# State space tiles: VectorE scales the rows of the next tile before it updates the state

## What is computed

```python
def ssd_scan(x, dt, a, bm, cm, h0, chunk):
    ...
    xd = (x.astype(f32) * dt[..., None])...
    acs = jnp.cumsum(la, axis=2)
    lmat = jnp.exp(jnp.where(incl[:, :, None, None], acs[:, :, :, None] - acs[:, :, None, :], -jnp.inf))
    cb = jnp.einsum('bcign,bcjgn->bcijg', cc, bc)
    y_diag = jnp.einsum('bcijgr,bcjgrp->bcigrp', cb[..., None] * lmat, xd)
    states = jnp.einsum('bcjgn,bcjgrp->bcgrpn', bc, xd * jnp.exp(acs[:, :, -1:] - acs)[..., None])
    def step(h, inp):
        s, d = inp
        return d[..., None, None] * h + s, h
    ...
    y_off = jnp.einsum('bcign,bcgrpn->bcigrp', cc, h_prev) * jnp.exp(acs)[..., None]
    return (y_diag + y_off)..., h_fin...
```

## Time and profile before

| | |
|---|---|
| median of 3 runs | 3017.64 us (3016.84 to 3018.11) |
| the profiled execution | 3013.33 us |
| its span | 3011.5 us |
| TensorE products busy | 2650.2 us, 88% of the span |
| VectorE busy | 1265.4 us, 42% |
| ScalarE busy | 940.2 us, 31% |
| GpSimd busy | 904.5 us, 30% |
| the stage of the state space tiles | from about 160 to 260 us |

### The profile page before, as it was taken

The page is one execution under the profiler, slowest core; times in us unless marked ns, Lnnn a source line. Parts: engine busy times, 40 slices in busy tenths (PEclk is TensorE's granted clock), DMA queues, the critical chain, the costliest instruction groups (busy, mean ns, idle before and its releaser), DMA issues. The chain is left out here.

```text
span 3011.5 us, 47221 instructions
## 1 busy us (share of the span) xinstructions
PE 2650.2 (88%) x19663; PEld 2397.8 (80%) x19663; DVE 1265.4 (42%) x2531; ACT 940.2 (31%) x1719; POOL 904.5 (30%) x449
## 2 busy tenths in 40 slices
PE   5778889988989999978878787879998889899998
PEld 5745888655889999977867686769996569899997
DVE  5764411576343222253755375442104552522224
ACT  4242221465352212152322333222214543412122
POOL 2241221133254333352233133213321003633331
PEclk9987989899999999988988898889999989999998
DMA  4202255441222222222201020102322172222221
GB/s 147 73 15 77 77 93 132 147 214 51 57 56 85 85 84 85 84 75 61 73 15 31 30 74 15 30 17 84 92 80 79 33 211 81 67 81 78 82 84 60
DMA packets 217570, 232.93 MB, mean 77 GB/s; under 512 B 40780, under 2 KB 186668, under 8 KB 216750
## 3 DMA queue, kind: packets, MB, share of 16 engines
q1 hardware_dynamic: 215278, 229.66, 24.9%
q10 hardware_dynamic: 2080, 0.25, 0.1%
HBM read 207.93 MB, written 48.35 MB: 85 GB/s over the span
## 5 line engine op out<-in xcount | busy, mean ns | idle before, releaser
L271 POOL TENSOR_TENSOR WRr<-WR,WH 128x2048 fp32r<-128x2048 f32 (+3 forms) x98 | 443.3, 4523 | 828.8 <-ACT WH L259 828.8
L2206 PE MATMUL PS<-HHr,WRr 128*128 128x288 f32 x1104 | 327.9, 297 | 0.0
L411 PE MATMUL PS<-HHr,WH 128*128 128x288 f32 (+1 forms) x928 | 278.3, 300 | 49.5 <-PEq L97 49.5
L411 PE MATMUL PS<-YTr,WRr 128*128 128x288 f32 x1024 | 304.4, 297 | 0.0
L259 ACT CAST WH<-WR 128x2048 fp32r<-128x2048 f32 (+3 forms) x98 | 180.5, 1842 | 347.3 <-DMA WR<-in_mlp_w 188.1
L411 PE MATMUL PS<-YTr,lt_WX 128*128 128x288 f32 x1408 | 281.8, 295 | 0.0
L411 PE MATMUL PS<-HHr,WRr 128*128 128x288 f32 (+1 forms) x928 | 277.8, 299 | 0.0
L411 PE MATMUL PS<-HTr,WH 128*128 128x288 f32 (+1 forms) x928 | 277.7, 299 | 0.0
L271 POOL TENSOR_TENSOR WRr<-WR,lt_WX 128x2048 fp32r<-128x2048 f32 x35 | 162.0, 4629 | 234.1 <-ACT lt_WX L259 234.1
L411 PE MATMUL PS<-WH,HHr 128*128 128x256 f32 (+3 forms) x760 | 220.8, 291 | 13.0 <-PEq L97 13.0
L411 PEld LDWEIGHTS PS<-YTr,lt_WX 128*128 128x128 f32 x1408 | 227.3, 189 | 0.1
(11 more groups left out here) (663 smaller groups left out, 6150.4 us busy)
## 6 DMA issues: line engine op xcount, KB each, us to landing
WR<-in_mlp_w SPq DMA_DIRECT2D x64, 1024.0 KB, 5.3
WR<-in_cd_w_in SPq DMA_DIRECT2D x34, 1024.0 KB, 5.4
out_dil_s<-in_cache_dil_kv SPq DMA_DIRECT2D x2, 7936.0 KB
WR<-in_ab_w_in SPq DMA_DIRECT2D x10, 1024.0 KB, 5.3
past_rows<-in_cache_nsa_kv SPq DMA_DIRECT2D x16, 256.0 KB, 3.4
WR<-in_ab_w_in SPq DMA_DIRECT2D x16, 256.0 KB, 4.2
WR<-in_nsa_ck_w SPq DMA_DIRECT2D x4, 1024.0 KB, 5.3
WR<-in_nsa_cv_w SPq DMA_DIRECT2D x4, 1024.0 KB, 5.7
```

Source lines behind the costliest of these rows:

```text
L271: pool.tensor_tensor(K.WRr[:, n % RING, 0:used], K.WR[:, n % RING, 0:used], high_slot(K, i, used).bitcast(F32), ALU.subtract).then_inc(K.l ...
L411: last = pe.matmul(out, a, b, start=(n == 0), stop=(n == 3 * len(terms) - 1))
L2206: last = pe.matmul(out, a[:, k, c], h[:, k, x], start=(n == 0), stop=(n == 3 * KT - 1))
```

## The change

In VectorE's loop over the tiles, the two calls at its end change places:

```diff
@@ -1217,8 +1217,8 @@
                         if t + 1 < TT:
                             times_cb(t + 1, 3)
                         if t < NT:
+                            rows(t + 1)
                             state(t)
-                            rows(t + 1)
```

## The result

The median went from 3017.64 to 3028.60 us, 7 runs each: a ratio of 1.0034 with a 95% interval of 1.0024 to 1.0044. The change makes the kernel slower, by 7 to 13 us, and the predicted 3027.3 lies 1.3 us from the median.

What follows compares the result with a forecast made beforehand. TensorE's order of work was taken to bound the state space tiles' stage. First pieces +9.12, second -5.75, clock +7.5 and last tile -1.2 gave +9.7 us, 3023.0 for the profiled execution and a median of 3027.3; range 3020 to 3034.

Steps and rivals of the forecast that it cites:

- The wait that takes over: TensorE's L1051 waits for the state (d_H), idle some 6.7 us in tile 1 and 7.9 in tiles 2 and 3.
- The first piece: From the transposes to the first masked product: 9.40 us in tile 1, 10.65 in tiles 2 and 3, together +9.12.
- The scalings: VectorE's two scalings and Btok take 4.32 us until its next instruction, VectorE starting ahead of GpSimd in every tile.
- The second piece: From the first masked product to the last broadcast sum: 4.45 us a tile at full clock, saving 5.75 us.
- The clock term: TensorE's clock falls to half in each gap of tiles 1 to 3, costing 2.50 us a tile, +7.5 us.
- Rival 1: The clock costs nothing new, as TensorE runs one dense burst after the wait: +2.2 us, 3019.8; chance 0.19.
- upper bound of 6.7 us a tile: Most the clock could cost each of tiles 1 to 3, if the period stays at half clock throughout.
- rival 3: The clock stays low from L1051 to each period's end in three tiles: +22.3 us, 3039.9; chance 0.12.
- The last tile: No L1051 waits for the state there, so scaling starts 0.43 us earlier and takes 0.80 less: -1.2 us.
- The sum: The stage's terms together, 9.12 - 5.75 + 7.5 - 1.2 = +9.7 us, giving a median of 3027.3 us.
- a change of time outside of the stage: Sign that the prediction is wrong: the change was to act in the state space tiles' stage only.

Runs made afterwards that it cites:

- e11: The changed kernel with GpSimd's d_YD waiting for Btok and unused products of ones in TensorE's gaps: 3010.48 us, ratio 0.9979.
- e10: The kernel before with GpSimd's d_YD waiting for Btok and unused products of ones in TensorE's idle time: 2999.41 us, ratio 0.9938.
- e2: The changed kernel with unused products of ones on TensorE behind the transposes, to hold the clock: 3017.61 us, ratio 0.9996 to the kernel before.
- e6: The changed kernel with GpSimd's d_YD waiting for Btok, not for the copied rows: 3024.77 us, ratio 1.0010 to the kernel before.
- e8: The changed kernel again, unaltered, for a second profile and more times: 3026.09 us, ratio 1.0018 to the kernel before.
- e1: The kernel before with the new order in the last tile only: 3022.50 us, ratio 1.0004.
- e3: The kernel before with unused products of ones in TensorE's idle time, to hold the clock: 3008.98 us, ratio 0.9970.
- e7: The kernel before with an added stage of four chained VectorE products behind the tiles, as a pause: 3032.87 us, ratio 1.0039.
- e4: The changed kernel with TensorE's first four masked products ahead of C times B in tiles 1 to 3: 3028.99 us, ratio 1.0033 to the kernel before.
- e9: The changed kernel with four masked products ahead of C times B and unused products of ones in TensorE's gaps: 3011.71 us, ratio 0.9973 to the kernel before.

## Why the prediction was right

**The wait that takes over** was right as put: L1051 waits for the state and names d_H, 6.66 and 7.92 us where 6.7 and 7.9 were forecast, and L1082's wait for Btok is gone but for the last tile. e11 against e10 shows it by itself.

**The first piece** was right to the tenth where the clock is full: 9.40 and 10.65 forecast, 9.33 and 10.62 in e2. The trace of the change has 10.64 and 11.93, the same with 1.3 us of half clock in it.

**The scalings** were right: VectorE first, L1185 1.23 and L1186 2.80 in tiles 1 to 4. The rule of the Trainium skill (SBUF — State Buffer, Who interferes with whom) agrees whoever starts first: VectorE's L1185 kept its 1.23 and d_YD stretched to 2.94 after the change, L1185 stretched to 2.63 and d_YD kept its 1.90 before. L1204 in e6, which started first and kept its 1.22, is one more case.

**The second piece** was forecast at -5.75 for the full clock. From the masked products to the last sum it is 4.34 in e2 in all three tiles, so -6.08 against the 4.45, 7.70 and 6.95 of before; in the trace of the change it is 4.74, 4.73 and 4.73, with some half clock in it.

**The clock term was mis-sized.** The sum had 2.50 us a tile, 7.5 in all; against e2 it was 1.71, 1.71 and 1.70, 5.1 in all, and 5.75 in e8. The 2.50 was read from tile 3 of before, where the clock came back only after the second group of masked products. After the change it is back within the first group (at about 191.9, 215.8 and 239.7), 3.5 us after L1051 began. What the Trainium skill says of idle gaps (TensorE: Matmul & The Clock Gate, HAM oscillation — how this bites in real kernels) agrees: behind the gap each burst starts at half clock, tile 1's new as well, with L1051 at 1.22 us instead of the 0.71 of e2.

Rival 1 held that L1051, a broadcast sum and the masked products, coming in one piece behind the wait, bring the clock back soon. That this was the reason is not shown: in e6 they come in one piece too, behind a gap of 6.34 us, and the clock was back only 4.9 and 5.9 us after L1051 began, in tiles 2 and 3, at a price of 2.40 and 2.84 us (periods of 23.00 and 23.45 against 20.60 and 20.61 in e11). So 2.50 is a price that this order of work can meet; why it was less after the change stays open.

The upper bound of 6.7 us a tile, on which rival 3 rests, was too low: it left out that VectorE's L1195 waits for TensorE's L1089. From the last sum to the end of L1089 it is 3.69 us in tile 1 before (192.26 to 195.95), and at half clock about 7.2 by an estimate from these rows, which would hold L1195 back by 2.6 us (it began 4.61 behind the sum) where the bound had 0.8: some 8.5 us a tile. No run kept the clock down for so long.

**The last tile** was right: -1.2 forecast, 17.29 - 16.08 = 1.2 measured between its transposes and L1296, and the same in e1.

**The sum** for the stage, with what was measured in its terms: +8.98 for the first pieces (9.33, 10.62 and 10.61 in e2 against 6.79, 7.75 and 7.04), -6.08, +5.12 for the clock and -1.21 make +6.8, which is what the stretch grew by; in e8 it grew by 7.5. The forecast said +9.7. The first measurement of the times has +11.0 (7.2 to 13.3), the second +3.4 by the medians and +5.4 by the ratio (0.6 to 10.0). Both intervals hold the forecast of 9.7, the first lies just above the 6.8 of the stretch and the second holds it, so the times can't tell the two apart. That 3027.3 came out 1.3 us from the median is luck: the stage brought 2.9 us less than forecast, and 4.1 us outside of it happened to come on top.

The prediction had named a change of time outside of the stage as a sign against it. The profiles show one: less the stretch, the span is 2931.8 us before, 2940.1 after and 2937.2 in e8. But it is 2943.2 in e1, 2936.3 in e3 and 2945.3 in e7, which keep the order of before in tiles 1 to 3, so the sign doesn't tell the change from other executions and doesn't count against the mechanism.

## What to carry to other kernels

When two pieces of work of one engine change places, ask for each which wait it ends and what stands ahead of the freed work in the queue of the engine that waits: here the masked products, which looked free to go, stood behind one that needed the state. Put the less urgent piece where its engine idles anyway, and take the time of the urgent one from what it contends with; one moved wait on GpSimd gave 6.6 us in the stage, and the swap lost 6.8. Judge changes of this size by a stretch of the profile, since the times of this kernel scatter by more.

## What the runs showed of the hardware that was not expected

- Products whose results nobody reads, put into TensorE's gaps, kept the clock of tiles 2 and 3 of the change at 1.00 where it was 0.79 (e2), and made the stage 8.3 us shorter in the order of before (79.66 to 71.32) and 8.4 in that of the change (86.48 to 78.06). They cost nothing where they ended before the wait did: in e2 L1051 starts 7.92 and 9.21 us behind the transposes, as without them.
- The length of a gap did not size its price. Gaps of 6.7 and 7.9 us cost the same in the first profile of the change, 1.7 us a tile, and 2.1 and 1.8 to 1.9 in e8, the same program; in e6 gaps of 5.1, 6.3 and 6.3 us cost 1.6, 2.4 and 2.8 (periods against e11). In tiles 2 and 3 of these three profiles the clock came back 3.5 to 5.9 us after the first products behind the gap had begun. In e4, where four heads of masked products stood in the gap alone, the following two sums took 3.42 us instead of 1.88 in e9.
- The whole time of the kernel before varied by 19 us over 26 runs on one chip (3012.1 to 3031.4). The stretch of the changed kernel was 86.48 and 87.12 us in its two profiles. One source of the spread is a part between 700 and 800 us that took 64.1 to 64.2, 71.0 or 71.8 us.
